# A hand-written order of steps in a two-block transformer kernel: the table of the first stage replaced by another one

## The reference

```python
h = rmsnorm(x); proj = h @ w_in            # gu, gv, q, k, v, gate, two logits
y_a = gelu(u) * (tril(W_s) @ LN(gelu(v)) + b_s)          # chunks of 128 tokens
q, k, v = silu(causal_dwconv(q, k, v)); q, k = l2norm(q), l2norm(k)
m = strict_lower(k_beta @ k.T * lmask)     # per head and chunk
sol = solve(I + m, [v_beta, k_beta * exp(decay)])        # triangular solve
for each chunk:                            # the recurrence
    v_new = u - w @ state; o = q_dec @ state + qk @ v_new
    state = state * cd + k_dec.T @ v_new
x = x + concat(y_a, rmsnorm(o) * silu(gate)) @ w_out
```

## Time and profile before

| | |
|---|---|
| median of three executions | 1544.95 us (1544.72 to 1545.86) |
| profiled execution | 1545.65 us |
| span in its profile | 1543.9 us |
| PE busy | 1533.8 us, 99% of the span, 8134 matmul records |
| DVE, ACT, POOL busy | 877.0, 607.7, 102.5 us |
| first stage (the table), on PE | about 26.6 to 276.6 us |
| granted TensorE clock | 0.999 of full speed |

### The profile page before, as it was taken

The page is one execution under the profiler, slowest core; times in us unless marked ns, Lnnn a source line. Parts: engine busy times, 40 slices in busy tenths (PEclk is TensorE's granted clock), DMA queues, the critical chain, the costliest instruction groups (busy, mean ns, idle before and its releaser), DMA issues.

```text
span 1543.9 us, 20409 instructions
## 1 busy us (share of the span) xinstructions
PE 1533.8 (99%) x8134; PEld 1269.9 (82%) x8134; DVE 877.0 (57%) x1336; ACT 607.7 (39%) x983; POOL 102.5 (7%) x87
## 2 busy tenths in 40 slices
PE   9999999999999999999999999999999999999998
PEld 7888889887788888888888887877888888888887
DVE  7777766644454353436566777544555653664565
ACT  6547334433343241323455343533244331332333
POOL 0000202110020000000130000100011000000000
PEclk9999999999999999999999999999999999999999
DMA  7121213521123223232322232222332232223212
GB/s 270 56 69 32 80 69 127 188 82 62 57 101 109 96 85 107 96 98 89 107 96 68 86 113 90 96 76 69 116 105 86 100 106 96 94 98 99 93 62 75
DMA packets 44861, 146.70 MB, mean 95 GB/s; under 512 B 4960, under 2 KB 8288, under 8 KB 44640
## 3 DMA queue, kind: packets, MB, share of 16 engines
q1 hardware_dynamic: 42592, 141.93, 27.4%
q10 hardware_dynamic: 2176, 3.47, 0.7%
HBM read 143.29 MB, written 2.10 MB: 94 GB/s over the span
## 4 chain that ended last, share of the span: by engine, by line
PE 97%; issue 1%; DVE 1%; DMA 0%; ACT 0%; SPq 0%; POOLq 0%; POOL 0%; DVEq 0%
PE bank L1237 29%; PE bank L1239 29%; PE bank L1238 29%; PE bank L1453 1%; PE bank L1470 1%; PE bank L1366 1%; PE bank L1392 1%; PE bank L1397 1%; PE bank L1487 0%; PE bank L1205 0%; PE bank L1207 0%; PE bank L1206 0%; PE bank L1510 0%; PE bank L1499 0%; DMA x_first<-x_in 0%
## 5 line engine op out<-in xcount | busy, mean ns | idle before, releaser
L1237 PE MATMUL bank<-a_hi,w_hi 128*128 128x512 f32 (+1 forms) x1275 | 497.6, 390 | 0.0
L1239 PE MATMUL bank<-a_hi,w_lo 128*128 128x512 f32 (+1 forms) x1275 | 490.4, 385 | 0.0
L1238 PE MATMUL bank<-a_lo,w_hi 128*128 128x512 f32 (+1 forms) x1275 | 490.1, 384 | 0.0
L1816 DVE TENSOR_TENSOR w_lo<-w_raw,w_hi 128x1024 fp32r<-128x1024 f32 (+2 forms) x259 | 328.1, 1271 | 146.6 <-ACT w_hi L1531 146.1
L1531 ACT ACTIVATE w_hi<-w_raw 128x1024 fp32r<-128x1024 f32 (+2 forms) x259 | 266.2, 1034 | 205.5 <-PE bank L1239 197.1
L1237 PEld LDWEIGHTS bank<-a_hi,w_hi 128*128 128x128 f32 x1275 | 239.8, 188 | 49.1 <-issue 2.4
L1239 PEld LDWEIGHTS bank<-a_hi,w_lo 128*128 128x128 f32 x1275 | 239.6, 188 | 48.0
L1238 PEld LDWEIGHTS bank<-a_lo,w_hi 128*128 128x128 f32 x1275 | 239.9, 188 | 45.6 <-issue 0.2
L1237 PE MATMUL bank<-b_hi,w_hi 128*128 128x512 f32 (+1 forms) x720 | 276.7, 384 | 0.0
L1239 PE MATMUL bank<-b_hi,w_lo 128*128 128x512 f32 (+1 forms) x720 | 275.4, 382 | 0.0
L1238 PE MATMUL bank<-b_lo,w_hi 128*128 128x512 f32 (+1 forms) x720 | 275.3, 382 | 0.0
(11 more groups left out here) (318 smaller groups left out, 1194.9 us busy)
## 6 DMA issues: line engine op xcount, KB each, us to landing
w_raw<-weights_in SPq DMA_DIRECT2D x247, 512.0 KB, 3.2
w_raw<-weights_in SPq DMA_DIRECT2D x8, 384.0 KB, 3.0
x_first<-x_in SPq DMA_DIRECT2D x8, 256.0 KB, 6.4
xs<-x_in ACTq DMA_DIRECT2D x2, 1024.0 KB, 10.0
w_raw<-weights_in SPq DMA_DIRECT2D x8, 256.0 KB, 2.7
mem_x<-mem_in SPq DMA_DIRECT2D x1, 1024.0 KB, 7.4
out<-xs SPq DMA_DIRECT2D x8, 128.0 KB, 1.8
w_raw<-front_in SPq DMA_DIRECT2D x5, 192.0 KB, 6.5
```

Source lines behind the costliest of these rows:

```text
L1237: pe.matmul(to, weights_hi[:, at], hi, start=k == k0, stop=False)
L1238: pe.matmul(to, weights_hi[:, at], lo, start=False, stop=False)
L1239: t = pe.matmul(to, weights_lo[:, at], hi, start=False, stop=k == k1 - 1)
L1816: dve.tensor_tensor(lo[:, 0:size], raw[:, n % SLOTS, 0:size], hi[:, 0:size].bitcast(F32), ALU.subtract).then_inc(split_dve.handle, 1)
```

## The change

Only the table `between` is replaced. The steps are the same ones, each once, with the same instructions. Their order is another one, and a projection may now be divided behind any input tile. The places where the new table has a level step of one head next to one of another head, and the places of which the prediction speaks, are shown:

```diff
-        ((8, 4, 8), [("split", 10), ("conv", 9), ("squared", 5), ("level_y", (0, 2)), ("mask", (0, 3)),
-            ("low", 10)]),
-        ((9, 0, 4), [("taps", 9), ("decay_exp", 1), ("norms", 1), ("level_x", (0, 2)), ("strict", 1),
-            ("level_y", (0, 3)), ("mask", (0, 4)), ("low", 11), ("gate", 2)]),
-        ((9, 4, 8), [("level_x", (0, 3)), ("turn", 1), ("conv", 2), ("squared", 1), ("late", 1),
-            ("level_y", (0, 4))]),
-        ((10, 0, 4), [("taps", 2), ("level_y", (1, 1)), ("level_x", (0, 4)), ("mask", (1, 1)), ("silu", 2),
-            ("level_x", (1, 1)), ("shape", 2), ("split", 12), ("level_y", (0, 5))]),
...
-        ((37, 0, 8), [("out", 3), ("b", (0, 2)), ("b", (0, 1)), ("b", (0, 0)), ("b", (0, 7)), ("mem_v", 0),
-            ("split", 41), ("low", 41)]),
-        ((38, 0, 8), [("b", (0, 6)), ("b", (0, 4)), ("b", (0, 5)), ("reload", 0), ("split", 42)]),
-        ((39, 0, 8), [("split", 43), ("low", 42), ("low", 43)]),
...
+        ((5, 1, 4), [("shape", 4), ("taps", 4), ("low", 7), ("rates", 1), ("decays", 0), ("sums", 4), ("decay",
+            0)]),
...
+        ((7, 0, 1), [("taps", 1), ("conv", 5), ("split", 9), ("turn", 0), ("shape", 1), ("mask", (0, 1)), ("shape",
+            5), ("low", 8), ("low", 9)]),
+        ((7, 1, 2), [("mask", (1, 5))]),
+        ((7, 2, 3), [("gate", 1), ("taps", 5)]),
+        ((7, 3, 7), [("squared", 5)]),
+        ((7, 7, 8), [("level_y", (0, 1))]),
+        ((8, 0, 3), [("sums", 5), ("late", 0), ("decay", 1)]),
+        ((8, 3, 6), [("decay_exp", 1)]),
+        ((8, 6, 7), [("squared", 0), ("level_x", (0, 1)), ("low", 10), ("gate", 2), ("mask", (0, 2)), ("sums", 1)]),
+        ((8, 7, 8), []),
+        ((9, 0, 1), [("mask", (0, 3))]),
+        ((9, 1, 4), [("norms", 1), ("level_y", (0, 2)), ("strict", 1), ("level_x", (0, 2)), ("mask", (0, 4))]),
+        ((9, 4, 6), [("split", 11), ("level_y", (0, 3)), ("turn", 1), ("level_x", (0, 3))]),
+        ((9, 6, 7), [("conv", 2), ("low", 11)]),
+        ((9, 7, 8), []),
+        ((10, 0, 4), [("late", 1), ("taps", 2), ("level_y", (0, 4)), ("level_y", (1, 1)), ("mask", (1, 1)),
+            ("level_x", (0, 4)), ("level_x", (1, 1)), ("split", 12)]),
...
+        ((12, 0, 1), [("shape", 6), ("taps", 6), ("level_y", (0, 5)), ("level_x", (1, 2)), ("silu", 1), ("level_x",
+            (0, 5)), ("sums", 2), ("split", 14)]),
+        ((12, 1, 2), [("conv", 10), ("level_y", (0, 6)), ("mask", (0, 6)), ("squared", 2), ("mask", (1, 2)),
+            ("sums", 6)]),
...
+        ((14, 2, 7), [("level_x", (1, 4)), ("strict", 2), ("decay_exp", 2), ("late", 2)]),
+        ((14, 7, 8), []),
+        ((15, 0, 1), [("level_y", (1, 5)), ("turn", 2), ("level_x", (1, 5))]),
...
+        ((19, 1, 3), [("statistics", 1), ("level_y", (2, 4)), ("level_y", (3, 1)), ("level_x", (2, 4)), ("split",
+            20), ("square", (1, 4))]),
...
+        ((20, 1, 7), [("level_y", (3, 2)), ("normalise", 1), ("low", 22), ("mask", (3, 2)), ("level_x", (2, 5)),
+            ("level_x", (3, 2))]),
...
+        ((30, 1, 8), [("state", 1), ("mix", 3), ("fresh", 2)]),
...
+        ((38, 0, 8), [("b", (0, 5))]),
+        ((39, 0, 8), [("b", (0, 6)), ("b", (0, 7)), ("b", (0, 4)), ("mem_v", 0), ("low", 42), ("low", 41), ("low",
+            43), ("split", 43), ("split", 41), ("split", 42)]),
```

More of the change, by code:

```diff
@@ L262, in schedule @@
[L262 to L288, removed]
@@ L296, in schedule @@
[L296 to L316, removed]
@@ new lines, in schedule @@
+        ((6, 0, 1), [("gate", 0)]),
+        ((6, 1, 2), [("taps", 8), ("norms", 0), ("strict", 0), ("decay_exp", 0), ("sums", 0)]),
+        ((6, 2, 3), [("split", 8)]),
+        ((6, 3, 5), [("split", 10)]),
+        ((6, 5, 8), []),
+        ((7, 0, 1), [("taps", 1), ("conv", 5), ("split", 9), ("turn", 0), ("shape", 1), ("mask", (0, 1)), ("shape",
[3 more added lines that the diff above has]
+        ((7, 3, 7), [("squared", 5)]),
@@ new lines, in schedule @@
+        ((13, 0, 1), [("keys", 0), ("level_x", (1, 3))]),
+        ((13, 1, 2), [("split", 15)]),
+        ((13, 2, 3), [("square", (1, 1))]),
+        ((13, 3, 4), [("conv", 3), ("taps", 3), ("level_y", (1, 4)), ("low", 14), ("taps", 10), ("decay", 2),
+            ("solve", 0), ("conv", 7)]),
+        ((13, 4, 7), [("shape", 10)]),
+        ((13, 7, 8), []),
+        ((14, 0, 1), [("low", 15)]),
+        ((14, 1, 2), [("mask", (1, 4)), ("norms", 2)]),
+        ((14, 2, 7), [("level_x", (1, 4)), ("strict", 2), ("decay_exp", 2), ("late", 2)]),
@@ new lines, in schedule @@
+        ((16, 3, 4), [("level_x", (1, 6)), ("low", 19), ("level_x", (2, 1)), ("square", (1, 0)), ("sums", 7),
+            ("square", (1, 2))]),
+        ((16, 4, 5), [("split", 17), ("level_y", (2, 2)), ("low", 17), ("decay", 3), ("shape", 3), ("solve", 1)]),
+        ((16, 5, 8), []),
+        ((17, 0, 3), [("squared", 7), ("low", 18)]),
+        ((17, 3, 5), [("spatial_v", 0), ("square", (1, 3)), ("mask", (2, 3))]),
+        ((17, 5, 7), [("spatial_u", 0), ("level_x", (2, 2)), ("sums", 3), ("statistics", 0), ("decay_exp", 3)]),
@@ new lines, in schedule @@
+        ((17, 7, 8), [("norms", 3)]),
+        ((18, 0, 2), [("level_y", (2, 3)), ("normalise", 0), ("split", 21), ("strict", 3)]),
+        ((18, 2, 5), [("late", 3), ("mask", (2, 5)), ("spatial_v", 1)]),
+        ((18, 5, 8), [("mask", (2, 4))]),
+        ((19, 0, 1), [("mask", (3, 1)), ("split", 22), ("low", 21), ("turn", 3), ("level_x", (2, 3))]),
+        ((19, 1, 3), [("statistics", 1), ("level_y", (2, 4)), ("level_y", (3, 1)), ("level_x", (2, 4)), ("split",
+            20), ("square", (1, 4))]),
@@ new lines, in schedule @@
+        ((22, 7, 8), [("stage", (1, 0)), ("stage", (1, 4))]),
+        ((23, 0, 4), [("level_y", (3, 5)), ("stage", (1, 1)), ("stage", (1, 6)), ("statistics", 3), ("stage", (1,
+            2)), ("solve", 2)]),
+        ((23, 4, 6), [("level_x", (3, 5))]),
+        ((23, 6, 8), [("normalise", 3), ("stage", (1, 3)), ("stage", (1, 5)), ("stage", (1, 7))]),
+        ((24, 0, 2), [("gate", 3)]),
+        ((24, 2, 3), [("row", 1), ("level_y", (3, 6)), ("level_x", (3, 6)), ("low", 25)]),
+        ((24, 3, 5), [("low", 27), ("split", 25), ("split", 27), ("mask", (3, 6))]),
```

91 lines of the change are left out of this document (80 added, 11 removed).

## The result

The change took 1547.30 us (median of 21 runs, 1545.46 to 1549.11) against 1544.84 for the kernel before on the same chip (21 runs, 1544.65 to 1546.14): a ratio of 1.0014, interval 1.0008 to 1.0021. It is 2.46 us slower, less than the 3.1 us that I had named as telling a change from none, but above my forecast of 1543.9 and just outside my range. Its runs scatter by 3.7 us, those of before by 1.5, and all but two of these by 0.6.

The account below looks back on a forecast made before the run. PE, busy 99% of the span, was taken as the bound. Visits and gaps -1.58, old waits -1.80 and new waits +2.21 gave -1.17 us, from 1544.95 to about 1543.8, rounded to 1543.9; 8-in-10 range 1541.9 to 1547.0.

Parts of the forecast that it names:

- Visits and gaps: PE's first stage: four fewer unbroken runs of 64x64 steps at 0.36 us, seven fewer gaps at 0.02; 1.58 us less.
- Waits inside the stage: PE's waits in the first stage: five old ones go, 1.80 us; new ones of 2.21 us come.
- `level_y (0, 3)`: Entry (9, 1, 4): `strict 1`'s DVE operations stand ahead of the subtraction this step needs; PE waits 0.51 us.
- `turn 2`: Entry (15, 0, 1): PE reaches it before DVE's start of the inverse after `strict 2` is ready; 0.61 us wait.
- ACT's copy: At (9, 4, 6), (10, 0, 4) and (19, 1, 3) one other step is too short to hide it: 0.28 us each, 0.84 together.
- The three doubtful places: `decays 0`, projection 8's bank and `fresh 2` at (30, 1, 8): taken at nothing, 0.5 us each kept for the range.
- point (4): Table's end: `split 43` ahead of 41 and 42 on ACT waits for projection 39; projection 41 starts 0.25 us late.
- Rival B: Thirteen gaps with level steps of two heads each pay 0.28 us for the copies out; 1546.6 us, chance 0.14.
- Rival C: DVE's strict chain meets PE in full at `level_y (0, 3)` and `turn 2`, 5.8 us for 1.12; 1548.5 us, chance 0.12.

Follow-up runs that it names:

- the repaired kernel: The changed kernel with `sums 5`, `level_y (0, 3)` and `turn 2` one input tile later, `low 39` ahead of `low 40`, splits 41, 42, 43 in order: 1542.21 us, ratio 0.9979.

## Why the prediction was wrong

**Visits and gaps: right.** The changed trace has 36 - 4 = 32 visits and seven gaps fewer (49 to 42 by its count, 51 to 44 by mine, which began earlier). The price is 0.35 to 0.36 per visit.

**Waits inside the stage: near in sum, partly elsewhere.** I had 0.51 for `level_y (0, 3)`, measured 0.32 (0.64 in place of 0.32 behind the large matmul); 0.61 for `turn 2`, measured 0.38 (0.89 less 0.51); 3 x 0.28 for ACT's copy, measured 3 x 0.18: the second step starts 1.16 behind the first, not 1.26 as I took it from the earlier trace rows, and 0.98 of that is work. `sums 5` (0.53) and projection 39 (0.45) I missed. The three doubtful places cost nothing. Without point (4), which lies behind the stage, my sum made it 1.17 + 0.25 = 1.42 us shorter; it is 1.2 shorter, and the measured waits (0.32 + 0.38 + 0.54 + 0.53 + 0.45 = 2.22) account for it: -1.58 - 1.80 + 2.22 = -1.16. That my sum came so near is partly luck: I had 0.72 too much at the places that I named and missed 0.98 elsewhere.

**The step that failed** stands under (4) and the doubtful places: "I found none whose landing comes within a projection of its use, so the order of DMAs costs nothing here". In (4) I had split 43 waiting for projection 39 alone, and 0.25 us of wait: the wait for its load was put at nothing. The order costs just that, 0.27, where load 43 is in time. In the change it lands 1.9 us after projection 39, because `low 39` is held up behind the reload and because the reload's bytes are then ahead of it on the DMA engines: 1.95 in the profile, in place of the 0.25. That alone turns the forecast of 1.2 us faster into 0.8 slower. The rest is argued. If in part of the runs the clock falls behind that pause, as it did in four profiles of edited kernels, it adds about 1.5 us: -1.2 + 2.0 + 1.5 is +2.3, and the median of +2.46 would lie among such runs. That the clock fell in runs of the change itself is inferred from their mean clock; no profile of such a run was taken. The size is not firm either: measured a second time, the change was 1.16 above before, with an interval (0.9999 to 1.0017) that takes in no difference.

**The rivals.** Rival B comes nearest in number, 1546.6 for 1547.30, but not in cause: the copies cost 0.18 at three places, not at thirteen. By the rule of the Trainium skill (TensorEngine Tiling (Array Packing), section PSUM Bottleneck) the copies out of the banks may set the pace once the products are packed; this trace shows them doing so in three places, and a visit of 80 records at 179.44 us with no wait in it. Rival C was the right sign at the wrong place: DVE's chain was met for 0.32 and 0.38.

## What to carry to other kernels

When a hand-written order is changed, follow each load as a chain of its own: what its issue waits for, which transfers are ahead of it, and which in-order queue passes its lateness on. A transfer started by another engine counts in that, and where it stands in the program does not fix when it is issued. A step that waits for such a load should stand last in its queue when its result is needed last: in the repaired kernel the load took longer than in the change, and nothing waited for it.

## What had not been expected of the hardware

- ACT issued a DMA up to 3 us ahead of activations that stand before it in the program (issued at 267.69 and 268.18, the last of them over at 270.82); with the reload behind the last splits it was held back by `split 43`, which waits for projection 39, and still went out (274.52) ahead of the two splits behind that one, over at 277.41.
- PE's granted clock fell to 0.50 behind pauses of 2.05, 3.14, 3.18 and 3.83 us in profiles, and stayed at 1.00 behind 1.82 and 1.95. By the mean clock of each microsecond it fell before the pause of 3.18 was over, and in the three others an estimated 0.3 to 1.3 us after PE had started again. What decides it between runs of one kernel is open: of the two kernels with pauses of some 3.1 us in their profiles, two of eleven runs each seem to have escaped, by their time and mean clock. The fall costs 1.5 to 1.6 us each time, whatever the length of the pause.
